# Projection tiles of the first layer on 512-column products, halves added on VectorE

## The reference

```python
q_a, c_kv, q_idx, k_idx, w_idx, q_b, k_b, v_b = jnp.split(x @ w_in, cuts, axis=-1)
o_a = dsa_attention(q_a, rms_norm(c_kv, kv_norm), q_idx, k_idx, w_idx * IDX_HEADS ** -0.5, w_uk, w_uv)
o_b = stick_breaking_attention(q_b, k_b, v_b)
x <- LN(alpha*x + concat(o_a, o_b) @ w_out);  x <- LN(alpha*x + SwiGLU(x))
```

## Time and profile before

| | us |
|---|---|
| median of 3 runs | 606.79 (606.64 to 607.08) |
| the profiled execution | 606.14 |
| its span, first to last instruction | 604.4 |
| TensorE products busy | 594.6 |
| VectorE busy | 417.9 |
| ScalarE busy | 340.4 |
| weight transfers, HBM read | 107.94 MB |

### The profile page before, as it was taken

The page is one execution under the profiler, slowest core; times in us unless marked ns, Lnnn a source line. Parts: engine busy times, 40 slices in busy tenths (PEclk is TensorE's granted clock), DMA queues, the critical chain, the costliest instruction groups (busy, mean ns, idle before and its releaser), DMA issues.

```text
span 604.4 us, 9813 instructions
## 1 busy us (share of the span) xinstructions
PE 594.6 (98%) x3475; PEld 513.6 (85%) x3475; DVE 417.9 (69%) x680; ACT 340.4 (56%) x633; POOL 24.6 (4%) x49
## 2 busy tenths in 40 slices
PE   8999999999999999999999999999999999999995
PEld 7989987788888888888888898888888888888884
DVE  5698657878665665665887888768776665666547
ACT  6775876366555455455556766646564555455530
POOL 1011111100000000000010000002000000000000
PEclk9999999999999999999999999999999999999998
DMA  8757426557656556555448533652775556555401
GB/s 315 252 178 262 140 87 202 166 188 232 228 187 198 175 184 206 181 189 189 139 133 256 199 130 121 210 182 79 261 244 192 181 187 208 197 177 183 137 1 69
DMA packets 30114, 109.45 MB, mean 181 GB/s; under 512 B 3377, under 2 KB 3377, under 8 KB 29953
## 3 DMA queue, kind: packets, MB, share of 16 engines
q1 hardware_dynamic: 28512, 102.77, 50.9%
q0 software_dynamic: 1568, 6.23, 3.1%
HBM read 107.94 MB, written 1.05 MB: 180 GB/s over the span
## 4 chain that ended last, share of the span: by engine, by line
PE 93%; DVE 4%; DMA 2%; ACT 1%; issue 0%; SPq 0%; DVEq 0%; ACTq 0%
PE bank L1142 25%; PE bank L1055 24%; PE bank L1058 13%; PE bank L1120 6%; PE bank L1534 4%; PE bank L1048 3%; PE bank L1528 2%; PE bank L1538 2%; PE bank L1098 2%; PE bank L1104 2%; PE bank L1097 2%; DVE wlo L702 2%; PE bank L1236 1%; PE bank L1247 1%; PE bank L1227 1%; DMA raw<-stream_in 1%
## 5 line engine op out<-in xcount | busy, mean ns | idle before, releaser
L702 DVE TENSOR_TENSOR wlo<-raw,whi 128x1024 fp32r<-128x1024 f32 x190 | 226.6, 1224 | 53.9 <-ACT whi L356 53.7
L356 ACT CAST whi<-raw 128x1024 fp32r<-128x1024 f32 x190 | 192.2, 1049 | 14.1 <-DMA raw<-stream_in 13.4
L1055 PE MATMUL bank<-hTs,whi 128*128 128x512 f32 x640 | 159.9, 392 | 0.0
L1055 PEld LDWEIGHTS bank<-hTs,whi 128*128 128x128 f32 x640 | 116.2, 189 | 21.6
L1058 PEld LDWEIGHTS bank<-hTs,wlo 128*128 128x128 f32 x640 | 87.3, 190 | 6.2
L1142 PE MATMUL bank<-whi,oThi 128*128 128x512 f32 x234 | 92.3, 394 | 0.0
L1142 PE MATMUL bank<-whi,oTlo 128*128 128x512 f32 x234 | 91.4, 390 | 0.0
L1142 PE MATMUL bank<-wlo,oThi 128*128 128x512 f32 x234 | 91.1, 389 | 0.0
L1058 PE MATMUL bank<-hTs,wlo 128*128 128x256 f32 x640 | 89.2, 282 | 0.0
L596 ACT COPY kT<-bank 128x256 f32<-128x256 f32 x40 | 14.9, 373 | 70.3 <-PE bank L1058 70.3
L951 DVE TENSOR_TENSOR kT<-bank,kT 128x256 f32<-128x256 f32 x40 | 16.9, 424 | 52.6 <-ACT kT L596 52.6
(11 more groups left out here) (176 smaller groups left out, 737.6 us busy)
## 6 DMA issues: line engine op xcount, KB each, us to landing
raw<-stream_in SPq DMA_DIRECT2D x190, 512.0 KB, 4.6
qT<-ln_rows_in POOLq DMA_DIRECT2D x8, 512.0 KB, 4.9
kT<-stream_in SPq DMA_DIRECT2D x2, 512.0 KB, 5.5
v<-xT_in SPq DMA_DIRECT2D x2, 512.0 KB, 5.5
h<-x_in POOLq DMA_DIRECT2D x1, 1024.0 KB, 7.5
out<-h SPq DMA_DIRECT2D x4, 256.0 KB, 2.1
dist<-consts_in POOLq DMA_DIRECT2D x1, 384.0 KB, 3.6
ukv<-w_uk_in POOLq DMA_DIRECT2D x1, 256.0 KB, 7.1
```

The costliest lines, as they stand in the source:

```text
L356: nc.scalar.copy(whi[:, c % RING, j * HW:(j + 1) * HW], raw[:, c % RAW, j * HW:(j + 1) * HW]).then_inc(whi_ready, 1)
L702: nc.vector.tensor_tensor(wlo[:, c % RING, cols], raw[:, c % RAW, cols], whi[:, c % RING, cols].bitcast(F32), ALU.subtract).then_inc(wlo_r ...
L1055: mm(dst[:], whi[:, slot, off + k * P:off + (k + 1) * P], hTs[:, k].rearrange("p j s -> p (j s)"), start=(k == 0), stop=False)
```

## The change

In chunks 1 to 3 each of the six tiles is formed by `halves_out` in a bank of its own (banks 5, 0, 4, 5, 4, 5), ScalarE copies the half from the low activations, scaled, and VectorE adds the other half, scaled, to it in SBUF. `proj_evac` loses three counts, so its later waits have other numbers for the same events. TensorE's waits on the banks become waits on VectorE's adds (`tile_evac`): the dots wait for the second, the fourth to sixth tile for the first, third and fourth, the first stick-breaking scores for the sixth. `cols_out` and `proj_half` are no longer called.

```diff
+        def early_bank(i):
+            return bank[(5, 0, 4, 5, 4, 5)[i]]
+        def early_place(i):
+            t, j = ((qiT, 0), (qiT, 1), (qT, 0), (qT, 1), (kT, 0), (kT, 1))[i]
+            return t[:, j, :], DH ** -0.5 if i in (2, 3) else 1.0
@@ ScalarE
+            def evac_early(i):
+                if i % 2 == 0:
+                    act.wait_ge(tile_done, i // 2 + 1)
+                else:
+                    act.wait_ge(chunk_used, 2 + i // 2)
+                dst, scale = early_place(i)
+                nc.scalar.activation(dst, early_bank(i)[:, S:2 * S], ACT.Copy, scale=scale).then_inc(tile_lo, 1)
             split_hi_half(2, 1)
+            evac_early(0)
             split_hi_half(3, 0)
-            evac_proj(1, 1, qiT)
             split_hi_half(3, 1)
+            evac_early(1)
             act.wait_ge(widx_done, 1)
             nc.scalar.activation(wq_i, ...)
+            evac_early(2)
...
             split_hi(4)
-            evac_proj(2, 2, qT[:, 0:2, :], DH ** -0.5)
-            split_hi(5)
+            evac_early(3)
+            split_hi_half(5, 0)
+            evac_early(4)
+            split_hi_half(5, 1)
             (ukT, cT)
-            evac_proj(3, 3, kT[:, 0:2, :])
+            evac_early(5)
@@ VectorE
-            for c in range(1, AHEAD):
-                split_lo(c)
+            def add_early(i):
+                dve.wait_ge(tile_lo, i + 1)
+                dst, scale = early_place(i)
+                nc.vector.scalar_tensor_tensor(out=dst, in0=early_bank(i)[:, 0:S], scalar=float(scale), in1=dst,
+                                               op0=ALU.mult, op1=ALU.add).then_inc(tile_evac, 1)
+            split_lo(1)
+            split_lo(2)
+            add_early(0)
+            split_lo(3)
+            add_early(1)
             dve.wait_ge(widx_ready, 1)
+            add_early(2)
...
             split_lo(4)
+            add_early(3)
...
             topk_round(0)
-            split_lo(5)
+            split_lo_half(5, 0)
+            add_early(4)
+            split_lo_half(5, 1)
             topk_round(1)
             topk_round(2)
             topk_round(3)
             split_lo_half(6, 0)
+            add_early(5)
             dve.wait_ge(vA_done, 1)
@@ TensorE
-            pe.wait_ge(wlo_ready, 1)
-            cols_out(bank[5][:, 0:S], 1, 0)
-            chunk(1)
-            cols_out(bank[5][:, S:2 * S], 1, KT * P).then_inc(chunk_used, 1)
-            proj_half(2, 2, 0, False)
+            def early_tile(i):
+                if i == 0:
+                    pe.wait_ge(wlo_ready, 1)
+                else:
+                    chunk(1 + i // 2)
+                if i >= 3:
+                    pe.wait_ge(tile_evac, (1, 3, 4)[i - 3])
+                last = halves_out(early_bank(i), 1 + i // 2, i % 2 * KT * P)
+                if i % 2 == 0:
+                    last.then_inc(tile_done, 1)
+                else:
+                    last.then_inc(chunk_used, 1)
+            early_tile(0)
+            early_tile(1)
+            pe.wait_ge(proj_evac, 1)
+            early_tile(2)
...
-            pe.wait_ge(proj_evac, 2)
+            pe.wait_ge(tile_evac, 2)
             for j in range(I_HEADS // 2):
                 dots(j)
-            proj_half(2, 2, 1, False)
-            proj_half(3, 3, 0, False)
+            early_tile(3)
+            early_tile(4)
...
-            proj_half(3, 3, 1, False)
+            early_tile(5)
...
             def stick_scores(m):
-                pe.wait_ge(proj_evac, 8 if m >= 2 else 4)
+                if m >= 2:
+                    pe.wait_ge(proj_evac, 5)
+                else:
+                    pe.wait_ge(tile_evac, 6)
```

More of the change, by code:

```diff
@@ L167, in build @@
             sem("glo_ready"), sem("ulo_ready"), sem("gsum_ready"), sem("usum_ready"))
+        tile_done, tile_lo, tile_evac = sem("tile_done"), sem("tile_lo"), sem("tile_evac")
         stored, rows_done = sem("stored"), sem("rows_done")
@@ L1110, in proj_quarter @@
                     chunk(c)
-                    if n >= 2:
-                        pe.wait_ge(proj_evac, n - 1)
+                    if n < 6:
+                        pe.wait_ge(tile_evac, n + 1)
+                    else:
+                        pe.wait_ge(proj_evac, n - 4)
                 dst = bank[4 + n % 2][:, half * S:(half + 1) * S]
@@ L1121, in proj_quarter @@
                 if half == 1 and part == 1:
[L1122 to L1135, removed]
                     last.then_inc(chunk_used, 1)
@@ L1348, in stick_values @@
             def stick_values(m):
-                pe.wait_ge(proj_evac, 10 if m >= 2 else 5)
+                pe.wait_ge(proj_evac, 7 if m >= 2 else 2)
                 pe.wait_ge(a_masked, 2 * m + 2)
@@ L1372, in moba_values @@
             def moba_values(j):
-                pe.wait_ge(proj_evac, 12 + max(j // 2 - 1, 0))
+                pe.wait_ge(proj_evac, 9 + max(j // 2 - 1, 0))
                 pe.wait_ge(probT_ready, A_HEADS + 2 * j + 2)
@@ L1392, in fill_l0 @@
                         if c == 10:
-                            pe.wait_ge(proj_evac, L0_OUT - 1)
+                            pe.wait_ge(proj_evac, L0_OUT - 4)
                     elif c == 10:
@@ L1398, in fill_l0 @@
                 elif c == 10 and half == 0:
-                    pe.wait_ge(proj_evac, L0_OUT)
+                    pe.wait_ge(proj_evac, L0_OUT - 3)
                 if (c, half) != (12, 1):
@@ L1421, in visit_l0 @@
                     j = S_AT[s]
-                    pe.wait_ge(proj_evac, 9 if j >= 2 else 6)
+                    pe.wait_ge(proj_evac, 6 if j >= 2 else 3)
                     if j == 0:
@@ L1499, in _ @@
             chunk(L1_IN + 1)
-            pe.wait_ge(proj_evac, 10)
+            pe.wait_ge(proj_evac, 7)
             both = slice((L1_IN + 1) % RING, L1_IN % RING + 1, RING - 1)
@@ L1508, in use_free @@
                 if i < 3:
-                    pe.wait_ge(proj_evac, 10 + i)
+                    pe.wait_ge(proj_evac, 7 + i)
                 elif L1_WHAT[USES[i - 3][0]][0] == "v":
-                    pe.wait_ge(proj_evac, 12 + L1_WHAT[USES[i - 3][0]][1] - 1)
+                    pe.wait_ge(proj_evac, 9 + L1_WHAT[USES[i - 3][0]][1] - 1)
                 else:
@@ L1565, in fill_l1 @@
                 elif q == 0 and half == 0:
-                    pe.wait_ge(proj_evac, 14)
+                    pe.wait_ge(proj_evac, 11)
                 if (q, half) != (2, 1):
```

## The result

The changed kernel takes 610.29 us (median of 17 runs, 607.51 to 612.72) against 606.79 (17 runs, 605.88 to 607.15): a ratio of 1.0062, 95% interval 1.0053 to 1.0071. It is slower, as forecast, but by 3.5 us instead of 2.0, outside the range, and its runs are spread over 5.2 us where those of before are spread over 1.3. The profiled execution took 611.79 us, 5.65 more than the one of before; it is one of the slower ones.

The account below looks back on a forecast made before the run. TensorE, busy 594.6 of 604.4 us, was taken as the bound. The 0.54 us tile gain and 0.25 us dots delay were held swallowed by the +1.97 wait at the scores: +2.0 on 606.79, 608.8 us, range 608.0 to 610.1.

Parts of the forecast that it names:

- Part 1: Six early tiles on TensorE: 2.79 us each instead of 2.88, 0.54 us gained; the skill's rule would give 0.1.
- tiles no faster: Third rival, chance 0.04: early tiles stay at 2.88 us, the first stick-breaking scores come later too, 609.1 us.
- Part 2: Evacuation of the tiles: ScalarE copies 0.37 us each, +0.45 in all; VectorE adds 0.42 each, +2.5 in all.
- Part 3: Wait ahead of the dots for the second add: TensorE stalls 0.52 us, dots start at 22.86.
- dots 0.25 later: Start of the indexer's dots: 22.86 instead of 22.61, behind VectorE's second add.
- Part 4: Fourth to sixth tile: no stall on their adds; the sixth tile has 0.7 us of cover.
- Part 5: Wait ahead of the first stick-breaking scores for the sixth add: start at 39.0 instead of 37.04, +1.97 us.
- it swallows the 0.25 of part 3: At the first stick-breaking scores: the stall absorbs the dots' 0.25 us delay and the tiles' 0.54, VectorE setting the place.
- Part 6: Behind the scores, through slots and norm: no idle time wins the delay back, so +2.0 us, 608.8.
- granted clock unchanged: Sign expected in the profile after: TensorE's granted clock stays as before despite the new waits.
- the fourth rival: TensorE's clock falls behind the 2.0 us stall at the scores, about 2.5 us more: 611.3; chance 0.04.

Follow-up runs that it names:

- both adds moved: Changed kernel, second tile's copy and add ahead of chunk 3's second half, sixth add between top-k rounds two and three: 606.26 us, ratio 0.9998; again 606.48 us, 0.9999.
- third trace of the changed kernel: The changed kernel with no further edit, measured a third time for comparison: 610.34 us (6 runs), ratio 1.0063.
- late parameters: Changed kernel with GpSimd's three parameter transfers issued only when chunk 3's second half has landed: 611.52 us (5 runs), ratio 1.0086.
- only the second add moved: Changed kernel with the second tile's copy and add put ahead of chunk 3's second half on ScalarE and VectorE: 608.64 us, ratio 1.0029.
- the changed kernel's second trace: The changed kernel with no further edit, run again for a second profile: 612.52 us (4 runs), ratio 1.010.
- late weights: Changed kernel, only the latent weights' two transfers held until chunk 3's second half landed, normed latent not waiting for them: 612.93 us, ratio 1.0102.

## Why the prediction was right and wrong

**Part 1, right.** A tile takes 1.84 + 0.95 us, as the earlier trace rows said (2.04 + 0.95 right behind the dots). In the kernel with both adds moved it is 23.02 and 23.01 us from the first tile to the scores, in the two traces of before 23.50 and 23.49: 0.48 us gained, of 0.54 forecast. The rule of the Trainium skill that part 1 weighed (same title and section) would have made it 0.1; the traces disagree with it here too. Chance "tiles no faster" 0.04: it didn't come.

**Part 2, right.** 0.37 to 0.39 us for ScalarE's copies and 0.41 to 0.42 for VectorE's adds.

**Part 3, the step that failed.** The path was right: from ScalarE's start on the landed half to the dots I had 22.86 - 20.18 = 2.68 us; it was 24.46 - 21.77 = 2.69, in the third trace of the changed kernel 24.42 - 21.73 = 2.69. The value put in was wrong: I took the landing in the one trace for a fixed time. ScalarE began on this half at 18.9 to 21.8 us in the fourteen traces, in both traces of the unchanged kernel at 20.2 and 21.1, in the three of the changed one at 18.9, 21.7 and 21.8. So the term "dots 0.25 later" is between -0.2 and 1.85 (22.43 and 24.46 against 22.61). The row that should have warned is the one I used: ScalarE's idle time "<-DMA" says that this operation starts when a transfer lands, and its time is no property of the program. Before, it had slack on TensorE's side until chunk 3 was needed; the change took the slack away. That this wait, with a late half, is what costs time is shown from both sides: the wait alone, put into the kernel before, costs 0.9 us, and without it the changed kernel loses 2.4 us less.

**Part 4, right.** No trace of the changed kernel has a wait ahead of the fourth to sixth tile. In the second one the fourth add ends at 29.56 and TensorE comes to the sixth tile at 30.39, a cover of 0.8 us for the 0.7 forecast. How thin that is, the kernel with late parameters shows: a wait of 2.3 us there.

**Part 5, right.** +1.97 forecast, +1.98 measured; a pause of 2.0 us in all three traces of the changed kernel, with landings nearly 3 us apart. The argument that the pause hangs on the end of L1316 and not on VectorE's backlog held there, not quite in the kernel with only the second add moved, where a late landing made VectorE's queue the longer path by 0.2 us. The path from the end of L1316 is 3.69 us, not 3.65: the 0.04 from that end (35.32) to ScalarE's start (35.36) are missing in the sum, but not in the 39.0.

But the sentence "it swallows the 0.25 of part 3" was wrong, by my own numbers: a path that starts at the end of L1316 moves with L1316, and that with the dots. Delay of the dots is added in full: 1.85 + 1.67 - 0.22 on L1316, then 1.98.

**Part 6, nearly right.** 5.28 at the scores was 4.98 at the norm and 5.68 at the end. The slots gave nothing back: the high part ahead of the norm (107.93 before) starts at 113.29, 5.36 later. The norm gave back 0.4, for which the sum had no term.

**The clock, the second step that failed.** The forecast had "granted clock unchanged", and the fourth rival 0.04 and a price of 2.5 us; I forecast, moreover, one long pause. Over the traces, the eleven pauses of 1.8 to 2.3 us in the opening were followed by the lower clock in four (this trace's first, the second of the changed kernel's second trace, the one ahead of the sixth tile with late parameters, the second with late weights), and in none of the openings without such a pause. At layer 1's entry, one pause of 2.3 us was followed by it and one of 2.5 us was not; behind waits of up to 1.6 us there is no fall in any trace. The cost was 1.5 to 1.7 us each time. The price of 2.5 was by the length of the warm-up, whose products took about as long as these at the lower clock, though its granted clock reads 1.00. The mechanism was named, its odds were guessed from the absence of rows; with no row on either side they should have been wide, and the range with them.

**The size.** With a landing as in the third trace of the changed kernel and full clock the scores start at 40.67, 3.6 us late; the span is 608.0 us, 3.6 more than in the trace of before, and the run took 609.79, 2.9 more than the median of before beside it. With an early landing the scores start 1.6 us late (38.62), and each fall of the clock adds 1.5 to 1.7. So the median of +3.5 fits a late landing with full clock or a middle one with one fall; that is an argument from three traces, not a count. How often the clock falls in the runs that have no trace is only hinted at by their mean clocks (0.990 to 0.999).

**Open.** What sets the landing of this half: it was late also without GpSimd's latent weights beside it. The transfer is issued at 14.0 to 14.2 and takes 4.7 to 7.7 us for the same bytes in different executions.

## What to carry to other kernels

When work is moved behind a wait for a transfer, treat the landing in one trace as one draw: find every queue in which it stands ahead of the new instruction, and ask what happens if it comes one or two microseconds later. Put an evacuation where its own input is ready, not behind the next prefetch: both places cost 2.4 us here, and moving the second copy and the two adds gives all of it back. A saving on the bound engine of 0.5 us isn't worth two new waits of 2 us on another engine's list, and a pause of that length can cost once more through the clock.

## What the runs showed of the hardware

A pause of TensorE of 2.0 us in the midst of dense work was followed, in some executions and not in others of the same program, by a stretch at 1.2 GHz (granted clock 0.50) that cost 1.5 to 1.7 us: five of the thirteen pauses of 1.8 to 2.5 us in the fourteen traces. Pauses of up to 1.6 us were followed by none. The Trainium skill (TensorE: Matmul & The Clock Gate, Why this matters for your kernels) advises against pauses between bursts of products, but only against longer ones than these; the traces here show that 2.0 us can be too long. A 512 KB transfer issued at the same point of the program landed up to 2.9 us apart from one execution to the next.
